# A hybrid decoder layer with 32 MoE experts: one weight chunk per light expert split in halves, and two weight loads issued earlier

## What is computed

```python
h = h + concat(o_gla, o_diff) @ w_out
x = rms_norm(h, norm2_g)
# router: softmax over 4 groups, top-1 group, then top-2 of its 8 experts, so 2 experts of 32 for each token
for e in range(32):                       # expert_block
    hdn = silu(xb @ w1[e]) * (xb @ w3[e]) # w1, w3: 1024 x 512
    y   = hdn @ w2[e]                     # w2: 512 x 1024
h = h + scatter_add(y * weight)           # for each token its two experts
```

## Time and profile before

| what | value |
|---|---|
| median of 3 runs | 1173.14 us (1172.59 to 1173.27) |
| the profiled execution's own time | 1172.78 us |
| its span in the trace | 1171.0 us |
| share of the span: PE, DVE, ACT, POOL | 95%, 75%, 59%, 29% |
| experts | from about 585 us to the end |

### The profile page before, as it was taken

The page is one execution under the profiler, slowest core; times in us unless marked ns, Lnnn a source line. Parts: engine busy times, 40 slices in busy tenths (PEclk is TensorE's granted clock), DMA queues, the critical chain, the costliest instruction groups (busy, mean ns, idle before and its releaser), DMA issues.

```text
span 1171.0 us, 17312 instructions
## 1 busy us (share of the span) xinstructions
PE 1115.4 (95%) x5838; PEld 860.2 (73%) x5839; DVE 879.3 (75%) x1298; ACT 695.1 (59%) x958; POOL 338.9 (29%) x394
## 2 busy tenths in 40 slices
PE   6999999999999989999699999999999999999997
PEld 5877887767777678888567777777777777777775
DVE  4424323666566788888679999999999999999995
ACT  5425202544455544434347777777777788888884
POOL 1211102321111221222463242323424245444211
PEclk9998999999999999999789999999999999999999
DMA  8130302110200263342589999999999999999992
GB/s 323 47 108 1 108 1 72 35 65 28 99 28 18 91 186 140 131 177 95 206 319 385 373 393 380 380 395 372 392 377 378 389 376 385 398 391 385 395 390 66
DMA packets 66912, 271.66 MB, mean 232 GB/s; under 512 B 12757, under 2 KB 19481, under 8 KB 42393
## 3 DMA queue, kind: packets, MB, share of 16 engines
q1 hardware_dynamic: 57000, 245.32, 53.8%
q0 software_dynamic: 6384, 19.14, 7.1%
q10 hardware_dynamic: 3456, 6.29, 1.4%
HBM read 246.74 MB, written 26.48 MB: 233 GB/s over the span
## 4 chain that ended last, share of the span: by engine, by line
PE 80%; DVE 10%; ACT 5%; issue 2%; POOL 2%; DMA 1%; ACTq 0%; POOLq 0%; SPq 0%; DVEq 0%
PE main_pm L693 13%; PE main_score L693 7%; PE main_score L2084 5%; PE main_score L2086 5%; PE main_score L2085 5%; DVE main_w_low L2054 4%; PE main_score L754 3%; PE main_pt L2086 3%; PE main_pt L2084 3%; PE main_po L2086 3%; PE main_po L2084 3%; PE main_pt L2085 3%; PE main_po L2085 3%; ACT main_w_high L2050 2%; PE main_pt L2096 2%
## 5 line engine op out<-in xcount | busy, mean ns | idle before, releaser
L2054 DVE TENSOR_TENSOR main_w_low<-w_raw,main_w_high 128x2048 fp32r<-128x2048 f32 x190 | 434.0, 2291 | 38.8 <-ACT main_w_high L2050 36.9
L2050 ACT CAST main_w_high<-w_raw 128x2048 fp32r<-128x2048 f32 x190 | 362.5, 1909 | 68.5 <-PE main_score L2086 52.2
L1953 POOL DMA_INDIRECT main_xg<-xn_dram,main_token x32 | 79.0, 2468 | 275.4 <-DVE main_token L1926 264.5
L2084 PE MATMUL main_score<-main_w_high,main_hT_high 128*96 128x512 f32 x256 | 102.6, 401 | 1.1 <-DVE main_hT_low L2345 0.6
L2086 PE MATMUL main_score<-main_w_high,main_hT_low 128*96 128x512 f32 x256 | 100.7, 393 | 0.0
L2085 PE MATMUL main_score<-main_w_low,main_hT_high 128*96 128x512 f32 x256 | 100.3, 392 | 0.0
L693 PE MATMUL main_pm<-slot_high,xh 128*128 128x512 f32 x208 | 87.7, 422 | 2.1 <-DVE slot_low L1404 2.1
L693 PE MATMUL main_pm<-slot_low,xh 128*128 128x512 f32 x208 | 82.9, 398 | 0.0
L693 PE MATMUL main_pm<-slot_high,xl 128*128 128x512 f32 x208 | 82.8, 398 | 0.0
L1998 POOL DMA_INDIRECT out<-main_y,main_dest x31 | 50.0, 1614 | 89.3 <-ACT main_y L2010 60.7
L1055 ACT ACTIVATE main_prob<-main_score,main_nmax 128x128 f32<-128x128 f32 (+7 forms) x64 | 47.6, 744 | 33.4 <-DVE main_nmax L1463 32.5
(11 more groups left out here) (375 smaller groups left out, 2615.9 us busy)
## 6 DMA issues: line engine op xcount, KB each, us to landing
w_raw<-in_moe_w SPq DMA_DIRECT2D x192, 1024.0 KB, 19.6
slot_raw<-in_w_in SPq DMA_DIRECT2D x12, 1024.0 KB, 7.3
main_x<-in_x SPq DMA_DIRECT2D x8, 512.0 KB, 11.2
slot_raw<-in_w_out SPq DMA_DIRECT2D x4, 1024.0 KB, 6.8
main_hx<-in_x SPq DMA_DIRECT2D x8, 512.0 KB, 3.9
out<-main_hx SPq DMA_DIRECT2D x8, 512.0 KB, 2.6
xn_dram<-main_xn SPq DMA_DIRECT2D x8, 512.0 KB, 2.8
gr_dram<-main_stage ACTq DMA_DIRECT2D x8, 256.0 KB, 2.0
```

The lines of the kernel that those rows point to most:

```text
L1953: nc.gpsimd.indirect_dma_start(xg[u][0:slots], None, s["xn2_dram"], bass.IndirectOffsetOnAxis(token[u][0:slots, 0:1], 0), bounds_check=bou ...
L2050: nc.scalar.copy(wh[slot(c, e)][:], raw[u][c // 2][:, c % 2, :]).then_inc(w_high, 1)
L2054: nc.vector.tensor_tensor(wl[slot(c, e)][:], raw[u][c // 2][:, c % 2, :], wh[slot(c, e)][:].bitcast(F32), ALU.subtract).then_inc(w_low, 1)
L2084: nc.tensor.matmul(out, x_hi, w_hi, start=start, stop=False)
```

## The change

It has three parts.

1. For experts 19 to 31 (every light step after the first) chunk 0 is split by halves: ScalarE makes the high part in two casts of 128 x 1024, and VectorE the low part in two subtractions of 128 x 1024, of which the first waits for the first cast alone (a new semaphore, `w_half`). TensorE still waits for the whole chunk.
2. SyncE issues step 1's chunks 2 and 3 ahead of its wait for the gathered rows; chunks 4 and 5 stay behind it.
3. The two loads on `gain_in` now count on `head_in`, whose waits rise from 128 to 160; this gives back the semaphore that part 1 takes.

```diff
@@ front stage
-    gain_in, head_in = sem("gain_in"), sem("head_in")
+    head_in = sem("head_in")
...
-            sp.dma_start(out_gain[:, i:i + 1], a[n].rearrange("a k -> k a")).then_inc(gain_in, 16)
+            sp.dma_start(out_gain[:, i:i + 1], a[n].rearrange("a k -> k a")).then_inc(head_in, 16)
...
-                dve.wait_ge(head_in, 128)
+                dve.wait_ge(head_in, 160)
...
-                dve.wait_ge(gain_in, 32)
+                dve.wait_ge(head_in, 160)
@@ stage_experts
+    w_half = sem("w_high_half_ready")
...
+    def high_by_half(act, e, r, u):
+
+        act.wait_ge(raw_in[u][0], 16 * (r + 1))
+        act.wait_ge(chunk_used, number(e, 0) - 2)
+        for half in range(2):
+            w = slice(half * D, half * D + D)
+            nc.scalar.copy(wh[slot(0)][:, w], raw[u][0][:, 0, w]).then_inc((w_half, w_high)[half], 1)
+
+    def low_by_half(dve, e, u):
+
+        for half in range(2):
+            if half == 0:
+                dve.wait_ge(w_half, e - HEAVY)
+            else:
+                dve.wait_ge(w_high, number(e, 0) + 1)
+            w = slice(half * D, half * D + D)
+            done = nc.vector.tensor_tensor(wl[slot(0)][:, w], raw[u][0][:, 0, w], wh[slot(0)][:, w].bitcast(F32),
+                                           ALU.subtract)
+        done.then_inc(w_low, 1)
@@ act_expert
-        if more:
+        if more and light[1]:
+            high_by_half(act, e + 1, pair(r, j, 1), 1 - u)
+        elif more:
             high(act, e + 1, pair(r, j, 1), 1 - u, 0)
@@ dve_expert
         if not (last and j == 3):
-            low(dve, e + 1, 1 - u, 0)
+            if light[1]:
+                low_by_half(dve, e + 1, 1 - u)
+            else:
+                low(dve, e + 1, 1 - u, 0)
@@ sync
+        for chunk in (2, 3):
+            load_chunk(sp, a, s, 1, 1, chunk, 1, 0)
         for u in range(2):
             sp.wait_ge(q.xg_in[u], 16)
-        for chunk in (2, 3, 4, 5):
+        for chunk in (4, 5):
             load_chunk(sp, a, s, 1, 1, chunk, 1, 0)
```

More of the change, by code:

```diff
@@ L2055, in low @@
                                 ALU.subtract).then_inc(w_low, 1)
-    def low_half(dve, e, u, c, half):
-        if half == 0:
-            dve.wait_ge(w_high, number(e, c) + 1)
-        w = slice(half * D, half * D + D)
-        done = nc.vector.tensor_tensor(wl[slot(c, e)][:, w], raw[u][c // 2][:, c % 2, w],
-                                       wh[slot(c, e)][:, w].bitcast(F32), ALU.subtract)
-        if half == 1:
-            done.then_inc(w_low, 1)
+    def high_by_half(act, e, r, u):
[14 more added lines that the diff above has]
+        done.then_inc(w_low, 1)
     def sp_expert(sp, e, r, j, last, light, tail=False):
```

## The result

The changed kernel is slower: 1193.18 us (median of 4 runs, 1184.83 to 1201.04) against 1173.20 us for the kernel before on the same chip, a ratio of 1.017 with a 95% interval of 1.010 to 1.024. The prediction gave 1171.2 us, a range up to 1174.0, and 8% to slower.

A forecast was written before the change was run, and what follows sets the result against it. It took the ScalarE-VectorE-TensorE loop of 16.90 us a light step as the bound, with VectorE and DMA close. Halves -2.3, early loads +0.4, gains nothing: -1.9 us, giving 1171.2 us, range 1169.5 to 1174.0.

The forecast's parts named there:

- So three resources stand within 4% of each other: Light steps: TensorE busy 16.35 of 17 us, VectorE 16.33, DMA share 1.02; a wait removed may fall to the next.
- the two paths behind it: ScalarE-VectorE-TensorE loop through chunk 0, 16.90 us without slack; second path through VectorE's low of chunk 5, 0.57 us behind.
- the rivals: Whole wait goes, 1169.9 (0.15); halves pay fixed part in full, 1172.4 (0.17); nothing gained, 1173.6 (0.10); slower, 1176.4 (0.08).
- the slower one: Rival, chance 0.08: first gather queues behind the two early loads, +5.6 - 2.3 = +3.3 us, 1176.4.
- The start of gate chunk 0, 0.49 us earlier.: First halved step: low of chunk 0 ends 0.49 us earlier, and TensorE's gate chunk 0 starts as much earlier.
- 0.20 us a step.: Steps 19 to 30 go from 16.90 to 16.70 us on average, 12 x 0.20 = 2.4 us; part 1 nets -2.3.
- the loop over two steps: Chunk 0, chunk 1, VectorE's whole step, TensorE: 33.80 to 33.40 us, with steps alternating about 16.5 and 16.9.
- The cost of two halves.: ScalarE's two casts 2.00 us against 1.92, VectorE's two subtractions 2.37 against 2.29; about half the fixed 0.16 hidden.
- VectorE's pause counted as slack.: Halves start earlier in VectorE's idle time before low of chunk 0; idle moves to low of chunk 1, 0.3 to 0.4 us.
- The weights.: Latest light-step load lands 3.65 us before use; about 2.2 is used up, so no wait, 1.4 us left.
- The early loads, +0.4 us.: Part 2 brings nothing, as no chain waits for these weights; it delays the first gather by 0.4, at most 5.6 us.
- The gains' edit.: Part 3 costs nothing: gains land by 32.7 us, first used at 67.4; it costs only if 34 us later.

The follow-up runs named there:

- halves_both_moves: Changed kernel without early loads; in light steps the scatter goes ahead of the gather and the targets between onehot and low of chunk 1; 1169.41 us, ratio 0.9976.
- halves_with_gap: Changed kernel, but VectorE's first half also waits for the whole high part, so its pause ahead of chunk 0 stays; 1174.33 us, ratio 1.0032.
- before_gap_filled: Kernel before, with an idle VectorE subtraction of 448 columns in the pause ahead of low of chunk 0 in light steps; 1171.82 us, ratio 0.9999.
- early_only: Kernel before plus only the early loads of step 1's chunks 2 and 3, without halves or the gains' edit; 1173.9 us, ratio 1.0024.
- targets_late: Changed kernel with the targets moved to the end of VectorE's light step; 1173.65 us, ratio 1.0014.
- halves_targets_late: Changed kernel without early loads, targets moved to the end of VectorE's light step; 1172.31 us, ratio 1.0003.
- before_later_filled: Kernel before, nothing halved; in light steps six one-column VectorE copies ahead of the token operation and an idle 192-column subtraction ahead of low of chunk 0; 1172.43 us, ratio 1.0005.

## Why the prediction was wrong, step by step

- **"So three resources stand within 4% of each other"**, and the two paths behind it: this is the step that failed. It looked at the turn of ScalarE, VectorE and TensorE and at the weights, and left out a fourth path: token, gather, scatter, the scatter's landing, targets, low of chunk 5. What the runs showed in its place: VectorE waits 21.0 us for late scatters and TensorE 18.9 us behind it, and either move that takes this wait out brings the time back, from 1190 us to 1170 to 1172. GpSimd is busy 8.07 of 17 us, which says nothing of its order. The path had 1.4 us of slack and lost it. None of the rivals held it; the slower one was the first gather, worth +5.6 at most.
- **The start of gate chunk 0, 0.49 us earlier.** Right: its waits fell from some 0.65 us to 0.15 to 0.28. The first step between two halved gate chunks took 16.71 us in the changed kernel, neither the shorter nor the longer that was forecast.
- **0.20 us a step.** The number came, by another path than the forecast's, and that is luck. Where the scatter is out of the way, steps take 16.72 us in most of halves_both_moves, against a forecast of 16.70 and 16.90 before, and the gain, 2.8 us (1.8 to 3.9), agrees with the forecast 2.3. But the loop over two steps would alternate 16.5 and 16.9, and the steps are even. A loop over one step sets them: ScalarE's high of chunk 0 and of chunk 1, VectorE's low of chunks 1 and 2 and the hidden rows, TensorE's down chunks, and the next high of chunk 0. The end of the hidden rows and the start of the down chunks, in the kernel before:

```profile
976.57 0.43 DVE L2345 TENSOR_TENSOR main_hT_low<-main_hT,main_hT_high 128x256 fp32r<-128x256 f32 x1
977.50 0.46 PE L2084 MATMUL main_score<-main_w_high,main_hT_high 128*96 128x512 f32 x1
```

  and in halves_both_moves:

```profile
993.39 0.43 DVE L2359 TENSOR_TENSOR main_hT_low<-main_hT,main_hT_high 128x256 fp32r<-128x256 f32 x1
994.04 0.46 PE L2096 MATMUL main_score<-main_w_high,main_hT_high 128*96 128x512 f32 x1 [0.17 <-DVE main_hT_low L2359]
```

  The hidden rows were ready 0.50 us ahead before and are ready 0.22 ahead now, with TensorE waiting for them: 0.28 us of slack. By the prediction's own numbers that gives 16.90 - 0.28 + 0.09 = 16.71. The prediction named this wait for step 31 alone.
- **The cost of two halves.** Right: casts 2.00 us for both, subtractions 2.35 where 2.37 was forecast and 2.29 is one piece. Of the fixed 0.16 us, 0.06 is paid; by the rule of "VectorE: DVE Perf Modes" in the Trainium skill, section "The TRN2 errata — SBUF-src ops pay a fixed extra latency per instruction", it would have been all, and this trace doesn't show it.
- **VectorE's pause counted as slack.** With the pause back (halves_with_gap) the gathers are short again, without halves it can be filled and they stay short (before_gap_filled). So it was slack for VectorE, and in the halved kernel not for GpSimd. VectorE's idle time did move to low of chunk 1, 0.45 to 0.65 us instead of 0.3 to 0.4.
- **The weights.** Not tested in the changed kernel, whose loads landed early. In halves_both_moves the forecast holds: no cast in the light steps waits for a DMA, and the loads issued from 1085 to 1094 us land after 26.5 to 27.6 us.
- **The early loads, +0.4 us.** Right in sign, undersized: early_only measured +2.8 us (1.4 to 4.1). Targets_late, with them, against halves_targets_late, without, makes it 1.3, on two chips. The first gather landed after 5.1 us against 4.33, so 0.8 of it is seen; where the rest goes stays open. "They bring nothing" holds.
- **The gains' edit.** No sign of a cost: halves_targets_late and halves_both_moves have it, at 1.0003 and 0.9976. It was never run alone.

## What to carry to other kernels

Before an operation is started earlier on a nearly full engine, write down the slack of every path through the queues it feeds, those of an engine that is half idle too: for each wait on a DMA's end, the issue, the landing and the moment of the wait. A short operation that waits for a far event should stand where its engine pauses anyway, and in a queue issued in order the transfer that someone waits for goes ahead of the one with time. The two moves here turned the halves' loss of 1.7% into a gain of 0.24%.

## What the runs showed of the hardware

A gather's issue on GpSimd ends with VectorE's operations. Before, low of chunk 5 ended at 965.58 + 2.29 = 967.87, and the gather, begun at 966.30, at 968.74: 0.87 later. In the changed kernel, VectorE around the gather that took 9.54 us and ended at 973.68:

```profile
963.26 2.28 DVE L2055 TENSOR_TENSOR main_w_low<-w_raw,main_w_high 128x2048 fp32r<-128x2048 f32 x1
965.46 2.35 DVE L2074 TENSOR_TENSOR main_w_low<-w_raw,main_w_high 128x1024 fp32r<-128x1024 f32 x2
967.73 0.68 DVE L1906 TENSOR_TENSOR main_onehot<-iota_slot,main_place_of 128x512 bf16<-128x512 f32 x1
968.33 4.48 DVE L2055 TENSOR_TENSOR main_w_low<-w_raw,main_w_high 128x2048 fp32r<-128x2048 f32 x2
972.74 0.41 DVE L2354 TENSOR_TENSOR main_hT<-main_score,main_slT 128x256 f32<-128x256 f32 x1
```

It ends 0.87 us behind low of chunk 2 (968.33 + 4.48 = 972.81), the last operation there with both inputs in SBUF before one that reads PSUM; five boundaries before it gave no way in. The lengths come in steps by which boundary lets it in: 2.3 to 2.5 us, 5.14 (a pause behind the onehot), 7.35 (the end of low of chunk 1) and 9.55; only the last light step's differ (4.5 or 6.7).

The Trainium skill has a rule near this, in "SBUF — State Buffer", section "SBUF: two separate sides": VectorE and GpSimd share a pair of ports by an exclusive lock, and while VectorE runs an operation in a two-port mode GpSimd can't write the descriptors of a DMA that it issues. For operations with two inputs in SBUF, such as the subtractions here, the page has the lock only against a GpSimd operation that reads SBUF; that a gather counts as one, it doesn't say. The ends in steps look like such a lock. The page's figure for how soon the DMA is let go behind VectorE's end, about 115 ns (section "A bandwidth-pool intuition that's wrong (but worth ruling out)"), isn't what is seen here: the gather's record ends 0.86 to 0.87 us behind. The prediction hadn't weighed that rule.

What stays open is why the boundary behind low of chunk 5 lets the gather in at one time and not at another. Two things go together in all long gathers. One is the halves without a pause in front. The other is lateness: the gather begins 0.13 us or more behind ScalarE's start on chunk 0, which a TensorE end releases. Neither makes them alone: targets_late has the halves, no gap and no lateness, and gathers of 2.27 to 2.58 us; before_later_filled is late by up to 0.29 us without halves, and has 2.51 to 2.55. Why the two together do it, no run shows. The place of low of chunk 5 and ScalarE's cast are spoken against by the runs above.

What such waits cost beyond their length is seen in the clock. In the changed kernel TensorE's waits of 4.65, 3.97, 3.83 and 1.82 us were followed by stretches with a granted clock under 1.00, those of 1.63, 1.52 and 1.50 us were not. So the longer of these waits cost more than they last.
